# A two-block transformer layer on one core: first expert's rows picked on TensorE instead of gathered, constant products in the router's waits, and the first FFN tiles in two halves of tokens

## The reference, cut to what matters

```python
h = _layer_norm(DEEPNORM_ALPHA * h + mix, ln1_g[l], ln1_b[l])
ffn = _hier_moe(h, w_rg[l], b_rg[l], w_re[l], b_re[l], w1[l], w3[l], w2[l])
...
grp = jnp.argmax(pg, -1)                      # group of a token
top_v, top_i = lax.top_k(le, MOE_TOPK)        # its two experts in that group
hb = jax.nn.silu(xb @ w1[e]) * (xb @ w3[e])   # per expert, on its rows
return hb @ w2[e]
...
hn = rmsnorm(h, norm2_g[l])                   # end of the second block
gu = hn @ w_ffn_in[l]
h = h + (jax.nn.silu(g) * u) @ w_ffn_out[l]
```

## Time and profile before

| | before |
|---|---|
| median of 3 runs | 2155.89 us (2151.8 to 2162.26) |
| the profiled execution's own time | 2162.86 us |
| its span in the profile | 2161.0 us |
| mean granted TensorE clock | 0.965 of full speed |
| PE busy | 1991.5 us, 92% of the span |
| DMA | 361.04 MB moved |

### The profile page before, as it was taken

How to read it: one execution, slowest core, us unless ns; L and a number is a source line. 1 busy time by engine, 2 the same in 40 slices (tenths; PEclk the granted TensorE clock), 3 DMA queues, 4 the chain that set the end, 5 groups by cost and what they waited for, 6 DMA issues and landing times.

```text
span 2161.0 us, 23359 instructions
## 1 busy us (share of the span) xinstructions
PE 1991.5 (92%) x9728; PEld 1455.5 (67%) x9728; DVE 919.1 (43%) x1409; ACT 660.8 (31%) x981; POOL 433.6 (20%) x310
## 2 busy tenths in 40 slices
PE   7999999999999889787787898999899999999999
PEld 6888878888877733333333347777666787888887
DVE  7674475542535622111111154445645884222332
ACT  4554432424333101000000132352236753222221
POOL 5432131423326011111111021311003220000121
PEclk9999999999999889898999999999999999999999
DMA  4861423123244599999999963111111134322210
GB/s 162 262 162 49 98 59 79 40 79 62 57 150 183 197 342 407 404 408 403 407 409 412 421 220 123 40 49 50 49 49 40 39 127 156 106 89 102 93 59 39
DMA packets 97655, 361.04 MB, mean 167 GB/s; under 512 B 9850, under 2 KB 34588, under 8 KB 85256
## 3 DMA queue, kind: packets, MB, share of 16 engines
q1 hardware_dynamic: 86800, 335.14, 43.2%
q0 software_dynamic: 8240, 19.00, 2.6%
q10 hardware_dynamic: 2504, 5.35, 0.7%
HBM read 338.74 MB, written 29.10 MB: 170 GB/s over the span
## 4 chain that ended last, share of the span: by engine, by line
PE 77%; DVE 13%; issue 5%; ACT 4%; DMA 1%; POOL 0%; ACTq 0%; SPq 0%; DVEq 0%; POOLq 0%
PE ps L272 73%; PE ps L276 3%; DVE ST L256 2%; PE ps L2094 2%; DVE H L262 1%; DVE WL L256 1%; ACT ST L268 1%; ACT L268 1%; DVE BG L262 1%; DVE ST L1005 1%; DVE BG L256 0%; ACT M L268 0%; DVE ML L256 0%; DVE H L256 0%; DVE M L256 0%
## 5 line engine op out<-in xcount | busy, mean ns | idle before, releaser
L272 PE MATMUL ps<-XH,WS 128*128 128x512 f32 x704 | 216.7, 389 | 0.0
L272 PE MATMUL ps<-HTH,WL 128*128 128x512 f32 x448 | 177.8, 397 | 0.0
L272 PE MATMUL ps<-W,BG 128*64 128x512 f32 x496 | 158.8, 614 | 1.0 <-issue 1.0
L272 PEld LDWEIGHTS ps<-XH,WS 128*128 128x128 f32 x704 | 132.2, 188 | 27.3
L266 ACT ACTIVATE BG<-ps 128x512 f32<-128x512 f32 x48 | 28.5, 595 | 386.3 <-PE ps L2094 338.8
L2201 DVE COPY BG<-ps 128x512 f32<-128x512 f32 x32 | 22.1, 692 | 287.6 <-PE ps L272 287.6
L272 PE MATMUL ps<-XL,WS 128*128 128x512 f32 x352 | 137.0, 389 | 1.4 <-DVE XL L256 1.4
L272 PE MATMUL ps<-X2H,GV 128*128 128x512 f32 (+1 forms) x512 | 130.8, 346 | 0.0
L272 PE MATMUL ps<-ST,BG 128*64 128x512 f32 (+2 forms) x416 | 102.6, 600 | 26.6 <-issue 25.8
L272 PE MATMUL ps<-M,BG 128*64 128x512 f32 (+1 forms) x304 | 119.8, 537 | 6.4 <-ACT ST L266 6.4
L272 PE MATMUL ps<-WS,HH 128*128 128x512 f32 x352 | 108.5, 389 | 0.9 <-DVE WS L256 0.9
(11 more groups left out here) (398 smaller groups left out, 4446.7 us busy)
## 6 DMA issues: line engine op xcount, KB each, us to landing
W<-in_w SPq DMA_DIRECT2D x31, 2048.0 KB, 39.4
W<-in_w_in SPq DMA_DIRECT2D x27, 2048.0 KB, 10.3
ST<-in_w SPq DMA_DIRECT2D x21, 2048.0 KB
BG<-in_w SPq DMA_DIRECT2D x11, 2048.0 KB, 33.6
U<-in_w SPq DMA_DIRECT2D x11, 2048.0 KB
M<-in_w SPq DMA_DIRECT2D x11, 2048.0 KB, 37.9
HT<-in_w SPq DMA_DIRECT2D x11, 2048.0 KB
W<-in_w_ffn_in SPq DMA_DIRECT2D x22, 1024.0 KB, 7.6
```

The lines of the kernel that those rows point to most:

```text
L272: return p.e.matmul(o, lhsT=l, rhs=r, start=start, stop=stop, skip_group_check=True)
```

## The change

Five things are edited.

1. `p_router` gives expert 0's transposed rows by 32 products: for each of 8 groups of features and 4 tiles of tokens, `H[:, i, k::8]` (tokens by 128 features, every eighth column) times `hot0[:, i, :]` (tokens by 64 rows, 1 where the token is that row of expert 0). DVE makes `hot0` with four more instructions. Expert 0 is not gathered; POOL starts with expert 1. The buffer counts and waits of `c_xg` and `CB0` are adapted.
2. The ninth expert load no longer waits for a gather.
3. `occupy` is called with 5 and 2 ahead of the last transposes and the last logits, with 5 ahead of `rank` and 4 ahead of `tok`.
4. `p_turn3(3)` moves from the end of `p_out` into the new `p_ffn_first`, and the two first FFN tiles are formed in halves of 256 tokens: the left half needs only the token tiles 0 and 1. Of the products before them, 5 constant ones are left and 3 dropped.
5. In `v_out`, the low halves of the token tiles 0 and 1 all stand ahead of the normalization of tile 3.

```diff
             p_logits(2)
+            t = B.tile(("lg", 3), 3)
+            room(t)
+            occupy(t, 5)
             p_turn("h1", H, 2, 3, (4, 5))
-            p_logits(3)
...
+            occupy(t, 2)
+            p_logits(3, t)
...
         def p_router():
+            first = B.tile(("ex", 0), 0)
+            room(first)
+            occupy(first, 5)
             t = B.tile("rank", 6)
...
             z.then_inc(t.filled)
+            occupy(first, 4)
             t = B.tile("tok", 7)
...
             z.then_inc(t.filled)
+            p.wait_ge(first_hot, 1)
+            for k in range(8):
+                for i in range(NT):
+                    z = mm(first.at[:, k * BLK:(k + 1) * BLK], H[:, i, k::8], hot0[:, i, :], start=i == 0, stop=i == NT - 1)
+            z.then_inc(first.filled)
...
                ALU.is_equal).then_inc(row_hot)
+            r0, eq = fc(16), hs[0].rearrange("p (n r) -> p n r", n=8)
+            stt(r0, c_rank, 1.0, mk[:, :, :, 0], ADD, MUL).then_inc(v.up())
+            v.wait_ge(*v.now)
+            ts(v, r0, r0, -1.0, None, ADD, None).then_inc(v.up())
+            v.wait_ge(*v.now)
+            tt(v, eq, io64.unsqueeze(1).to_broadcast([P, 8, BLK]),
+               r0.rearrange("p c i -> p (c i)").unsqueeze(2).to_broadcast([P, 8, BLK]), ALU.is_equal).then_inc(v.up())
+            v.wait_ge(*v.now)
+            tt(v, hot0, eq[:, 0:4, :], eq[:, 4:8, :], ADD).then_inc(first_hot)
             cnt = RT[:, 5, 128:160]
...
         def p_experts():
-            p_expert_x(0)
             for b in range(NE):
...
-            for b in range(NR):
+            for b in range(1, NR + 1):
                 g_gather(b)
-            for b in range(NE):
+            for b in range(1, NE):
...
             p_turn3(NT - 2)
-            p_turn3(NT - 1)
...
             v_low3(1, 0)
-            v_rms3(3)
             v_low3(0, 1)
             v_low3(1, 1)
+            v_rms3(3)
...
+        def p_ffn_first():
+
+            tiles, o = [B.tile(("gu", 0, y), y) for y in range(2)], fi_buf(0)
+
+            def add(y, z, ks):
+                for k in ks:
+                    i = exact(tiles[y].at[:, z], (o[0][:, k, y, :], o[1][:, k, y, :]), (XH[:, k, z], XL[:, k, z]), k == 0, k == 7)
+                return i
+
+            left, right = slice(0, 2 * P), slice(2 * P, T)
+            room(tiles[0])
+            occupy(tiles[0], 5)
+            p.wait_ge(fi_lo, 1)
+            for h in range(2):
+                for i in range(2):
+                    p.wait_ge(*B["x3", i, h].free())
+            add(0, left, range(4))
+            p_turn3(NT - 1)
+            add(0, left, range(4, 8))
+            room(tiles[1])
+            add(1, left, range(8))
+            for i in range(2, NT):
+                for h in range(2):
+                    p.wait_ge(*B["x3", i, h].free())
+            for y in range(2):
+                add(y, right, range(8)).then_inc(tiles[y].filled)
...
-            w_room[N_EXP + EXP_SLOTS.index(8)] = [(ln_hi, 12), (c_xg[0], 16)]
+            w_room[N_EXP + EXP_SLOTS.index(8)] = [(ln_hi, 12)]
```

More of the change, by code:

```diff
@@ L1665, in p_merge, with p_logits @@
             p_logits(2)
+            t = B.tile(("lg", 3), 3)
+            room(t)
+            occupy(t, 5)
             p_turn("h1", H, 2, 3, (4, 5))
-            p_logits(3)
-        def p_logits(i):
-            t = B.tile(("lg", i), i)
-            room(t)
+            occupy(t, 2)
+            p_logits(3, t)
+        def p_logits(i, t=None):
+            if t is None:
+                t = B.tile(("lg", i), i)
+                room(t)
             p.wait_ge(c_r, 128)
@@ L2063, in build @@
         hs = [flatK[:, 3072 + 512 * j:3584 + 512 * j] for j in range(2)]
+        hot0, first_hot = hs[1][:, 0:NT * BLK].rearrange("p (i r) -> p i r", i=NT), sem("first_expert_one_hot")
         yb = [flatV[:, 1024 * j:1024 * (j + 1)] for j in range(NR)]
@@ L2089, in p_expert_x @@
             j = b % NR
-            p.wait_ge(c_xg[j], 16 * (b // NR + 1))
+            p.wait_ge(c_xg[j], 16 * (b // NR + (j > 0)))
             t = B.tile(("ex", b), b % 2)
@@ L2382, in build @@
         xs = (X2H, X2L)
-        c_cb, CB0 = c_xg, 16 * NE // NR
+        c_cb, CB0 = c_xg, [16 * NE // NR - 16 * (i == 0) for i in range(NT)]
         c_hs, xn_done = c_h0, sem("xn")
@@ L2416, in p_rows_c @@
             p.wait_ge(dg_done, 8)
-            p.wait_ge(c_cb[i], CB0 + 32)
+            p.wait_ge(c_cb[i], CB0[i] + 32)
             for h in range(2):
@@ L3375, in p_turn3 @@
                 room(t)
-                if i == NT - 1 and h == 0:
-                    occupy(t, 5)
                 p.wait_ge(n2_done, i + 1)
@@ L3487, in v_split_in @@
             tt(v, fi_buf(n)[1], fi_raw(n), fi_buf(n)[0].bitcast(F32), SUB).then_inc(fi_lo)
+        def p_ffn_first():
[21 more added lines that the diff above has]
+                add(y, right, range(8)).then_inc(tiles[y].filled)
         def p_ffn_in():
-            for n in range(NF):
+            p_ffn_first()
+            for n in range(1, NF):
                 o = fi_buf(n)
@@ L3494, in p_ffn_in @@
                     room(t)
-                    if n == 0 and y == 0:
-                        occupy(t, 3)
-                        x3_parts(p)
                     p.wait_ge(fi_lo, n + 1)
@@ L3692, in _ @@
             w_room[N_EXP + EXP_SLOTS.index(6)] = [B["lg", i].full() for i in range(NT)]
-            w_room[N_EXP + EXP_SLOTS.index(8)] = [(ln_hi, 12), (c_xg[0], 16)]
-            w_room[N_SEC + 1] = [(c_cb[i], CB0 + 32) for i in range(NT)]
+            w_room[N_EXP + EXP_SLOTS.index(8)] = [(ln_hi, 12)]
+            w_room[N_SEC + 1] = [(c_cb[i], CB0[i] + 32) for i in range(NT)]
             w_room[N_SEC + 2] = [gr_read[1], gr_read[2]]
```

## The result

The changed kernel takes 2166.32 us (median of 18 executions, 2161.62 to 2170.51). The kernel before, run beside it, takes 2160.61 us (median of 18, 2151.8 to 2166.77). The ratio is 1.0029, with a 95% interval of 1.0017 to 1.004: the change costs 6.2 us (3.7 to 8.6). A gain of 6.7 us, to 2149.2 us, had been forecast. The median of before has itself moved up from the 2155.89 us of three executions, so that the same gain would now read 2153.9. The profiled execution of after has an own time of 2166.03 us, 3.2 above that of before.

What follows compares the result with a forecast made beforehand. PE was taken to bound the kernel, except where it waits for the experts' weight stream and at the FFN's start. Gains of 4.0 and 2.7 us sum to 6.7: 2149.2 us against the 2155.89 median, range 2141 to 2160.

Steps and rivals of the forecast that it cites:

- the price of the 64 one-hot records: Router: expert 0's one-hot products take 7.5 us at full clock, chosen between bounds of 7.5 and 14.4 us.
- 1.4 us: First expert's first products: run at full clock, 7.02 us instead of 8.43, gaining 1.4 us.
- The sum of the stream: Experts' weight loads: tenth load issued 4.0 us earlier, from 2.6 us earlier first expert products and 1.4 us shorter ones.
- Five of them (10 records) take 2.3 us: Router, ahead of the last transposes: first batch of five constant products at full clock, from 741.81 to 744.1.
- the cover of the gather for expert 1: Router: expert 1's rows, gathered later behind `hot0`, still land in time, with 3 to 5 us of cover.
- the stream moves with the first expert: Experts: tenth and eleventh loads wait for the first expert's first products; each us sooner moves everything behind.
- the ninth load gains nothing by itself: Experts' loads: freed, it follows the eighth at 749.24 and fills the hole around 763, with no gain alone.
- The FFN's start: First two FFN tiles: halves of 256 tokens end at 1803.2 instead of 1805.9, gaining 2.7 us.
- rival (4): FFN halves: products cost 0.2 us instead of 0.12, losing 7.7 us, time 2157; chance 0.02.
- rival (2): Router: one-hot products slow throughout, by half clock or strided weights; 2156.1 us, or 2160 to 2162 with half-clock batches; chance 0.13.
- its own first form: Router: one-hot products take 14.4 us, 6.9 more, batches at full clock; stream 2.9 later, FFN 2.7 back, 2156.1 us.
- Rival (1): Router: clock falls at some point, costing 1.5 us; stream gain 2.0 to 2.5, time about 2151; chance 0.26.

Runs made afterwards that it cites:

- blocks: Changed kernel with contiguous 128-feature blocks as one-hot weights, expert 0's `w1` and `w3` loaded in matching row order; 2165.87 us, ratio to before 1.0022.
- after_filled: Changed kernel with two more constant products in PE's wait for `hot0`; executed once, for its profile, 2169.82 us.
- rows_first: Changed kernel with one-hot operands exchanged: `hot0` as weights, `H` streaming 512 columns, then copy and four transposes; 2150.61 us, ratio to before 0.9956.
- halves_only: Kernel before with only the FFN token halves and the DVE reordering, router unchanged; 2158.19 us, ratio to before 0.9988.
- blocks_filled: blocks with two more constant products in PE's wait for `hot0`; 2162.06 us, ratio to before 1.0006.
- gather_const: Changed kernel with expert 0 gathered again and the ninth load waiting for that gather; constant products and halves stay; 2157.92 us, ratio to before 0.999.
- gather_const_ninth: gather_const with the ninth load no longer waiting for the gather; 2161.21 us, ratio to before 0.9999.
- step4: Changed kernel with every fourth column of `H` as one-hot weights, giving expert 0 wrong columns; executed once, for its profile, 2171.24 us.

## Why the prediction was wrong

**The step that failed** is the price of the 64 one-hot records: "I take 7.5, because the constant products and these keep PE nearly filled". Measured were 15.49 us, beyond the far bound of 14.4. Two of the prediction's own signs of being wrong came with it: a 128x64 record of 0.2 us or more, and a clock of 0.5 in the router. Two things were wrong in the step.

The first is the weights' step. The row that was used to dismiss it, the transposes at L2094 with 0.144 us a record, read every eighth column too, but for 64 rows, and the runs show that it does not carry over to these products of 128: 0.24 us at steps of 4 and 8, and half of it or less at steps of 1 and 2, all at clock 1.00. Besides, that row stood at clock 0.50, where contiguous records of blocks cost some 0.22 and strided ones 0.24, so that a step can hardly be seen there. The same 8 transposes at clock 1.00 were in the trace of before:

```profile
774.75 1.09 PE L2094 MATMUL ps<-cst,BG 64*128 64x64 f32 x8
```

They took 1.15 us at 0.50 and 1.09 at 1.00, while the logits' records went from 0.225 to 0.114. A price that the clock does not change is what the one-hot products show too, and this pair of rows could have warned. (Which part of the distance from 0.14 to 0.24 is due to the rows and which to the kind of product, no run separates.) The rule that spoke against the change (the Trainium skill, "Advanced Engine Details and Errata", SBUF Cachelines) stood beside it with the right result. The two bounds should have been left standing as equals.

The second is the clock. "Nearly filled" did not hold it: it fell to 0.50 two microseconds into the narrow products in after, and in after_filled, with no gap even ahead of them, after six. With the strided weights the fall costs the products nothing, since 0.24 us is their price at either level; but the first expert then began at 0.50 and took 8.43 us. The **1.4 us** that the prediction gave for it was lost too.

**The sum of the stream**, forecast 4.0 us earlier, came 6.7 later. The 10.7 us between are: the products 15.49 for 7.5, 8.0; the first expert 1.4; and 1.35 on the way to `hot_r`. There, "Five of them (10 records) take 2.3 us" was right only at full clock. The clock had fallen behind the narrow logits, as the earlier trace rows showed for before, and the batch stood in just that place: 4.09 us. `hot_r` was 0.25 us later and not 1.1 earlier. The chain of four DVE instructions (1.6 forecast, 1.47 measured) and the cover of the gather for expert 1 held.

**That the stream moves with the first expert** held in every run: SP's eleventh load went out at 781.09 in after, 778.58 in blocks and 767.75 in rows_first, in the order of the first expert's products, and in after the DMA engines were empty for 8 us ahead of it. The experts' last products (1255.15 to 1258.80 us in before), taken behind the logits' start, came 5.7 us later than before in after, 2.0 later in blocks and 6.5 earlier in rows_first; the two gathering kernels, whose first expert ended as before, had them 2.2 and 2.6 later, which is how well one profile tells this. That the ninth load gains nothing by itself held as well.

**The FFN's start** was right in mechanism and size: 2.96 us in after, 2.7 forecast, 2.6 (0 to 5.4) by halves_only's ratio. Its one unforeseen row is a wait of 0.40 us for `XL` ahead of the constant products. The halves' products cost 0.12 us each; rival (4) did not happen, and the rule of the Trainium skill, "TensorE: Matmul & The Clock Gate", Part 3, that the prediction set beside it (weight loads that do not overlap products in the same row groups) is not borne out by these 0.12 us.

**The rivals.** What happened is rival (2), at 0.13, by the second of its causes (the strided weights; half clock set in as well but did not make these products longer) and with the batch at half clock. It put that case at 2160 to 2162 us, 4 to 6 us above the median that it started from; measured are 6.2. Part of this match is luck: its own terms, 2156.1 and 2.3 for the one batch ahead of the transposes, give 2158.4. Against its own first form (stream 2.9 us later) the trace has 3.8 more: 1.1 in the products, 1.35 in the batch and 1.4 in the first expert, which it should have counted, since a clock that falls in the products is still down behind them. Rival (1) happened as well, as a part of it. As one could have seen, a fall in the router was not an event of chance 0.26: before shows one at the same narrow records.

**What stays open.** By the traces after should lose 3.8 us and blocks 0.5, and blocks_filled should gain 5.4; the ratios say a loss of 6.2 (from 3.7), of 4.8 (from 1.5), and of 1.3 (from a gain of 2.8 to a loss of 5.6). Some 4 us of blocks and 7 of blocks_filled are thus in neither stretch. The traces show where such time can lie: from the second expert's transposes (774.75 in before) to the 16 ahead of the FFN it takes 1011.3 us in before, 1011.6 in after, 1014.3 in blocks, 1014.0 and 1014.2 in the profiles of blocks_filled, 1015.4 in gather_const, 1011.2 in gather_const_ninth, and 1009.0 to 1009.7 in the three kernels with rows first, though no product in it is edited. In both profiles of blocks_filled over 3 us of this are lost in the 45 us behind the experts' last products. Part of what rows_first gains beyond its trace (9.5 us for 8.0) is there as well. Whether the edits shift this stretch or it moves by itself, one profile a kernel does not tell; the stretch ahead of the router, which no edit touches, already differs by 5 us (the 32 logit records start at 735.42 to 740.38).

## What to carry to other kernels

A gather by one-hot products pays where a load stream waits for it, if the one-hot matrix is the weight and the data streams: rows_first does in 16 records and 3.65 us what weights read with a step did in 64 and 15.49, and a copy and four transposes that come on top end 1.4 us later. Before strided weights are used, look whether a second element of each 16 bytes is read; a permuted load of the other operand makes them contiguous (what that load costs by itself was not measured). A row at half clock does not tell what a step costs at full clock: compare rows at both. Put filling products ahead of work that is to run at full clock, but not in the wait right behind narrow products: there they themselves ran at half clock, and pushed the path back by what they gained.

## What the hardware showed

- Products of 64 columns with full-height float32 weights (128 rows, 128 columns) read with a step of 8 floats take 0.24 us a record, at clock 1.00 and at 0.50 (after, after_filled), and with a step of 4 the same (step4); contiguous ones 0.115 at 1.00 (blocks_filled) and some 0.22 at 0.50 (blocks: 64 in 12.01 us, of which 2.1 us at 1.00 hold 18 at 0.115, so 46 in 9.9). Transposes with weights of 64 rows and a step of 8 took 0.14 at either level (before: 8 in 1.15 us at 0.50 and in 1.09 at 1.00).
- The clock fell from 1.00 to 0.50 in narrow products (36 and 64 columns) that followed each other without a gap on PE, at 759 in blocks and at 762 in after_filled, and in neither profile of blocks_filled. A fall behind the 36-column logits was there in all kernels but gather_const_ninth, whose first batch took 2.40 us.
- A gather of 64 rows took 6.63 to 7.42 us from issue to landing in three profiles in which the ninth load waited for it, and 7.95 in the one in which that load ran beside it.
